# Routing of the first token block in 8 work units instead of 16, of the second with its row products in 64 instead of 56, and the wait for a zero fill moved behind other work

## The reference, cut to what matters

```python
q = (xt @ w_q).reshape(T, PEER_HEADS, 2, PEER_HALF)
s = jnp.einsum('thpd,hpkd->thpk', q, sub_keys)            # 8 heads x 2 x 128 keys a token
sv, si = lax.top_k(s, 16)
cand = sv[:, :, 0, :, None] + sv[:, :, 1, None, :]        # 16 x 16 candidates a head
top, f = lax.top_k(cand, 16)
experts, gates = (i1 * 128 + i2), softmax(top)            # 128 picks a token
h = gelu(einsum('tkd,td->tk', u[experts], x))             # u, v: 16384 rows of 1024
out = einsum('tk,tkd->td', gates * h, v[experts])
```

## Time and profile before

| | |
|---|---|
| median of 3 runs | 2676.51 us (2668.55 to 2679.03) |
| the profiled execution | 2672.81 us, its span 2671.0 us |
| PE busy | 2488.9 us, 93% |
| DVE busy | 2032.5 us, 76% |
| ACT busy | 1162.2 us, 44% |
| POOL busy | 991.8 us, 37% |
| the chain that ended last | PE 53%, DVE 23%, "issue" 11%, DMA 7%, ACT 3% |
| DMA over the span | 684.60 MB, mean 256 GB/s |

### The profile page before, as it was taken

One profiled execution on the slowest core, in us unless ns is written; L12 is line 12 of the kernel. 1 busy time (PEld: TensorE's weight loads), 2 busy tenths in 40 slices (PEclk: granted clock), 3 DMA queues, 4 the chain that ended last, 5 costly groups with the idle time before them and its releaser, 6 DMA issues.

```text
span 2671.0 us, 44784 instructions
## 1 busy us (share of the span) xinstructions
PE 2488.9 (93%) x16674; PEld 2408.7 (90%) x16674; DVE 2032.5 (76%) x3708; ACT 1162.2 (44%) x1933; POOL 991.8 (37%) x667
## 2 busy tenths in 40 slices
PE   6998998889999899999999899898999999999997
PEld 6978998889999889999999799798999999999997
DVE  3544687889987499999965467789898955777764
ACT  3444543335466333333344545333363743333332
POOL 0012007878783123333020210378888801222200
PEclk8999999999999999999999999999999999999998
DMA  7395259986966999999843633699869589999871
GB/s 311 118 303 180 89 185 367 353 280 146 235 161 197 329 403 391 381 394 377 306 166 120 148 114 133 239 345 359 236 169 231 131 278 360 349 336 353 330 281 68
DMA packets 303733, 684.60 MB, mean 256 GB/s; under 512 B 87696, under 2 KB 219664, under 8 KB 258512
## 3 DMA queue, kind: packets, MB, share of 16 engines
q1 hardware_dynamic: 218880, 496.32, 53.5%
q0 software_dynamic: 84688, 186.16, 22.5%
HBM read 595.36 MB, written 86.64 MB: 255 GB/s over the span
## 4 chain that ended last, share of the span: by engine, by line
PE 53%; DVE 23%; issue 11%; DMA 7%; ACT 3%; POOL 1%; SPq 1%; DVEq 0%; POOLq 0%; ACTq 0%
PE ps L1096 19%; PE ps L1037 16%; PE ps L869 10%; DVE u_lo L1756 5%; DMA act_scratch<-act_h 4%; DVE u_rows_s L1768 2%; DVE acc_s L2021 2%; DVE v_lo L1996 2%; DVE mod_p L2062 2%; DMA act<-act_scratch 2%; PE ps L891 1%; PE ps L1061 1%; ACT u_hi L1318 1%; DVE w L2005 1%; PE ps L976 1%
## 5 line engine op out<-in xcount | busy, mean ns | idle before, releaser
L1037 PE MATMUL ps<-h_lo,u_hi 128*128 128x320 f32 x2048 | 648.7, 317 | 70.6 <-DVE u_lo L1756 61.3
L1096 PE MATMUL ps<-w_hi,v_lo 128*128 128x320 f32 (+1 forms) x2048 | 642.8, 314 | 40.8 <-DVE v_lo L1996 36.4
L1096 PE MATMUL ps<-w_hi,v_hi 128*128 128x320 f32 x2048 | 636.5, 311 | 0.0
L1096 PE MATMUL ps<-w_lo,v_hi 128*128 128x320 f32 x2048 | 636.5, 311 | 0.0
L1037 PE MATMUL ps<-h_hi,u_hi 128*128 128x320 f32 x2048 | 635.9, 311 | 0.0
L1037 PE MATMUL ps<-h_hi,u_lo 128*128 128x320 f32 x2048 | 635.8, 310 | 0.0
L751 POOL DMA_INDIRECT gate_scratch<-scat x256 | 514.3, 2009 | 87.7 <-issue 75.3
L1388 ACT CAST v_hi<-wring 128x1024 fp32r<-128x1024 f32 x256 | 268.5, 1049 | 510.1 <-PE ps L1096 504.3
L1037 PEld LDWEIGHTS ps<-h_lo,u_hi 128*128 128x128 f32 x2048 | 387.2, 189 | 95.3 <-DVE u_lo L1756 80.0
L1096 PEld LDWEIGHTS ps<-w_hi,v_lo 128*128 128x128 f32 x2048 | 387.9, 189 | 52.5 <-issue 34.5
L1996 DVE TENSOR_TENSOR v_lo<-wring,v_hi 128x1024 fp32r<-128x1024 f32 x256 | 313.0, 1223 | 156.4 <-ACT v_hi L1388 156.3
(11 more groups left out here) (275 smaller groups left out, 3548.6 us busy)
## 6 DMA issues: line engine op xcount, KB each, us to landing
wring<-in_u_t_dram SPq DMA_DIRECT2D x128, 1024.0 KB
wring<-in_v_t_dram SPq DMA_DIRECT2D x128, 1024.0 KB
act_scratch<-act_h SPq DMA_DIRECT2D x256, 160.0 KB
gate<-gate_scratch SPq DMA_DIRECT2D x64, 640.0 KB
act<-act_scratch SPq DMA_DIRECT2D x64, 640.0 KB
wring<-in_w_ada_dram SPq DMA_DIRECT2D x24, 1024.0 KB
mod_w<-in_w_mod_dram POOLq DMA_DIRECT2D x24, 1024.0 KB, 7.8
wring<-in_w_in_dram SPq DMA_DIRECT2D x20, 1024.0 KB
```

Of the source, the lines that this page charges most:

```text
L1037: last = nc.tensor.matmul(ps[:, 6 + s % 2, 0:TD], u[:, s % 2, k], hx[:, k, 0:TD], start=(k == 0 and n == 0), stop=(k == KC - 1 and n == 2))
L1096: last = nc.tensor.matmul(ps[:, half * (KC // 2) + c, cols], v[:, of % 4, d], w[:, group * G + of, cols], start=(opening and k == 0), stop ...
```

## The change

`ROUTE_LEN` goes from (16, 56, 24) to (8, 64, 24): the first block's remaining labels have 8 splits between them, one to two labels, and the second block's 24 labels have 64. `TB_AT` follows, the other constants are derived. The dots no longer start with the split of step 2 of the second block (two there, then one a step with a second one at every sixth); they start with step 6 and go evenly over 58 steps, one a step with a second one at steps 15, 25, 34, 44, 54 and 63. POOL's wait for the zero fill moves from before `o_evac` to right before the first additions, behind the first 16 gathers.

```diff
-ROUTE_LEN = (16, 56, 24)
-TB_AT = (0, 2, 10)
+ROUTE_LEN = (8, 64, 24)
+TB_AT = (0, 1, 10)
...
-ROUTE_DOTS = tuple((s >= 2) + (s % 6 == 5) + (s == 2) for s in range(ROUTE_LEN[1]))
+DOTS_FROM = 6
+ROUTE_DOTS = tuple((s + 1 - DOTS_FROM) * SLOTS // (ROUTE_LEN[1] - DOTS_FROM) - max(s - DOTS_FROM, 0) * SLOTS // (ROUTE_LEN[1] - DOTS_FROM)
+                   if s >= DOTS_FROM else 0 for s in range(ROUTE_LEN[1]))
...
-            pool.wait_ge(nought_st.sem, nought_st.at(l, 32 * PIECES))
-            pool.sem_inc(pool_passed.sem, 1)
             pool.wait_ge(o_evac.sem, o_evac.at(l, NU))
             pool.sem_inc(pool_passed.sem, 1)
             pool.dma_start(sk_0[:], subkeys_t[l, 0]).then_inc(sk_ld.sem, 16)
...
+            pool.wait_ge(nought_st.sem, nought_st.at(l, 32 * PIECES))
+            pool.sem_inc(pool_passed.sem, 1)
             for half in range(2):
                 cells_in_two(half)
```

## The result

The changed kernel takes 2692.97 us (median of 12 executions, 2682.44 to 2707.87) against 2676.93 for the kernel before beside it: ratio 1.007, 95% interval 1.0056 to 1.0083. It is slower by 16 us; the forecast was 2674, and its range ended at 2688. The profiled execution took 2682.44 (span 2680.6) and was the fastest of the twelve. Its span is only 9.6 us longer than the span before, so part of the loss isn't in it.

What follows compares the result with a forecast made beforehand. PE was taken as the bound, kept waiting in places by DVE's work. Terms -9.0 - 20.6 + 25.1 - 2.8 + 2.0 + 3.2 = -2.1 us took the median from 2676.5 to about 2674; range 2660 to 2688.

Steps and rivals of the forecast that it cites:

- First block in 8 units: First block: DVE decides, 47.8 us for 8 units instead of 28.2; +25.1 us over both layers.
- First dots: Second block: DVE's wait for gathered rows before the first dot goes, -10.8 and -9.8, together -20.6 us.
- Residue: Second block: unexplained 5.5 and 1.9 us (restarts, clock, store waits) carried over, 1.0 a layer added; +2.0 us.
- Label stalls: Second block: PE's stalls behind long routing pieces and second dots, 19.3 us before, 17.9 after; two layers -2.8 us.
- Clock: First block: PE's idle waits lower its clock, 1.6 us a layer at the last unit; +3.2, between 0 and 5.2.
- Rival 1: Second block: DMA is the real bound and work is only conserved; +24 us, 2700; chance 0.12.
- rival 2: Second block: gathers spread over more units relieve the stores, residue and clock cost vanish; -14.7 us, 2662; chance 0.11.
- rivals 3 and 4: 3: POOL's sk_0 issue stalls anyway, +9.0 us, chance 0.05; 4: rows late for first dots, +10 us, chance 0.07.
- Zero fill: Layer 0 before unit 0: POOL's additions end earlier, PE idles 0.9 us, not 8.01; with 1.7 of clock, -9.0 us.
- Behind the second block: Gate units after the second block: no change counted, 0 us.
- Profiled execution to median: Whole kernel: the median lies 3.7 us over the profiled execution, so 2670.7 becomes about 2674.

Runs made afterwards that it cites:

- e14: Kernel after with thin gathers (each moves an eighth of the row) and a ring of 8 gathered rows instead of 16; 2663.99 us.
- e1: The kernel after, unchanged, run and profiled once more; 2696.09 us, ratio 1.0084 to the kernel before.
- e3: Kernel after with the zero fill's wait back at its old place, so only the new unit split and later dots; 2702.01 us.
- e8: Kernel after with 104 extra matmuls a layer, results unused, filling PE's waits in the first block; 2701.01 us.
- e12: Kernel after with thin rows: each gather moves 512 bytes a partition, an eighth of the row, read eight times by the dot; 2679.53 us.
- e16: Kernel after, whole rows and ring of 16, first 16 gathers in two halves: the ninth waits until unit 15 is split; 2685.53 us.
- e4: Kernel before (16 and 56 units, fill's wait at its old place) with dots from step 6 of the second block; 2686.48 us, ratio 1.0041.
- e2: Kernel before with only the wait for the zero fill moved; 2668.07 us, ratio 0.9976.
- e18: Kernel before (16 and 56 units) with the fill's wait moved and dots from step 4, 16 gathers in a row, not halved; 2656.71 us.
- e5: Kernel after with a ring of 8 gathered rows instead of 16; 2685.49 us, ratio 1.0038.
- e7: Kernel before (16 and 56 units) with the fill's wait moved, dots from step 6 and a ring of 8; 2672.78 us, ratio 0.9981.
- e17: Kernel before (16 and 56 units) with fill's wait moved, dots from step 4, first 16 gathers in two halves (ninth waits for unit 22's split); 2654.48 us.
- e10: e2 with gathers from the fifth on spaced, each waiting for a further 0.75 unit to be split; 2688.64 us, ratio 1.0053.

## Why the prediction was wrong

The median is 19 us over the forecast. Unit 0 comes 3.5 us later than forecast, units 0 to 72 take 3.3 more in the two layers (298.7 for 299.1, 299.2 for 295.5), the gate units behind them 2.4, all the rest of the span 2.5, and the median lies 10.5 over the profiled execution, not 3.7: 6.8 more. Step by step:

- **First block in 8 units, +25.1: right.** The 8 units took 47.9 us, the forecast was 47.8; with 8 units at the floor it makes 76.1, as e14's unit 16 shows (76.2 and 76.1). DVE decides there.
- **First dots, -20.6: right as far as it went.** DVE's wait is gone and the rows were there in time. (The first gather starts 6.9 us behind the end of the staging; the 7.1 of the text counts from the start of its last copy, and the sum uses 6.9.) But before, PE stood still for much of the time in which the 16 gathers ran; now it runs on beside them, and what that costs was left to the residue.
- **Residue, +2.0: the step that failed**, at "I carry these over and add 1.0 a layer". 6.5 and 2.9 us were set aside for clock, restarts and stores. With thin rows and a ring of 8 the 64 units take 241.0 (e14), in the profiled execution of the kernel after 250.8 and 251.3: the gathers' bytes and their row cost 9.8 and 10.3, which is 10.7 more in the two layers than was set aside. In e1, e3, e8 and e12 units 12 to 16 take 21.6 to 24.6 us in six of eight layers, where the first profile has 18.5. Between the medians of the kernel after and e14 lie 29 us: 13.4 go with the bytes (to e12) and 15.5 with the row (e12 to e14), or, the other way round, 7.4 with the row (to e16) and 21.5 with the rest. By e4 the later dots alone, with what they bring, are 10.8 us slower.
- **Label stalls, 17.9 a layer: too many.** 241.0 is 15.7 over the floor of 225.3. This and the clock hid 7.6 of the 10.7. The sum also slips: three times 1.17 is 3.5, which makes 18.1 and a term of -2.4.
- **Clock, +3.2: nothing.** The granted clock was 0.86 and 0.93, but unit 8 came when DVE let it, with PE kept busy too (e8). The rule of the Trainium skill weighed there (TensorE: Matmul & The Clock Gate, HAM oscillation) does show: the granted clock of these eight units is under 1.00 in both layers, and in e1 matmuls behind a wait take 0.63 us instead of 0.31. In the first block it has no price.
- **Rival 1** had the right sign and the right place, the DMA engines beside the first gathers, but not by conserved work: the 64 units took 251 us and not the 264 it gives. PE's late counts it didn't have at all. Of the others, rival 2 had the sign wrong, and rivals 3 and 4 did not come: POOL's wait went, and the rows were in time.
- **Zero fill, -9.0: 5.5** in the profiled execution (unit 0 at 327.7, before 333.2), 6.3 in e2, 7.6 in the medians. The wait went; the seven additions took 2.5 us longer, and the 1.7 of clock was not won.
- **Behind the second block, 0: +2.4.** The double dot at step 63 makes the first gate units 1.2 us a layer longer.
- **Profiled execution to median, 3.7: 10.5.** The profile shown was the fastest of twelve. Units 12 to 16 of layer 1 took 18.5 us in it and 24.6 in e1's, so late counts that differ between executions may be why; for the executions without a profile it isn't shown.

The Trainium skill (DMA: Bandwidth & Descriptors, Issuing engines are not separate DMA queues) has the DMAs of all queues interleave on the same 16 engines. The trace agrees for the stores: with an eighth of the gathered bytes ACT's waits for them went from 41.4 us to none in layer 0. It says nothing of PE's counts, which stayed late with an eighth of the bytes.

**What stays open.** Why PE's count comes late. By more than 1 us it came late only while, or right after, a row of gathers was issued, by more with 16 in a row than with 8, whatever they move. A row of 16 isn't enough for it, since e18 and one layer of e2 and e4 have one and no late count, and a row of 8 doesn't rule it out (e5, e7). PE also pauses inside units ("issue", 0.95 to 1.31 us) near such places, so the count may be late because PE itself is held up in a way the profile doesn't show; or it has to do with the recording, since all these profiles lack updates. A kernel with 8 and 64 units and 16 in a row with a whole trace would decide that, and there is none. Nor is it shown why units 10 to 13 of the kernel after are hit in every profile and units 19 to 21 of the kernel before in half of them.

## What to carry to other kernels

A wait that stands where a burst of transfers runs may be what protects the other engines from it: before taking it away, ask what would run beside the burst, and try fewer bytes or a shorter burst at the same time. That isn't always a win: halving took 7.4 us off the kernel after (e16) and nothing with 16 and 56 units (e17 against e18), and spacing cost 20.6 where rows then came late (e10). Move such work by small steps and time each: the dots from step 4 win 11 us over step 2 (e18 against e2), from step 6 they lose 10.8 (e4). And run the changed kernel more than once before believing its profile: here the first one was the fastest of twelve.

## What the hardware did that I had not expected

- PE's semaphore count reached ACT up to 12.3 us after PE's last matmul (e8, unit 11 of layer 1), in every profile of a kernel with 16 indirect DMAs in a row behind the short first block, also when each moved only 64 KB (12.2 and 15.4 us a layer, e12), and up to 2.7 us with 8 in a row (e5). All profiles that show it lack some semaphore updates, so a part of the recording in it is not ruled out.
- The same seven additions on POOL took 10.32 us where PE, DVE and ACT worked beside them, and 7.81 where PE and DVE stood still. Busy time of that stretch in the kernel after (DVE 6.52, ACT 6.18 of 10.4 us), then of two of its additions, one beside ACT alone, one beside PE, DVE and little of ACT:

```profile
234.50:244.90 10.40, 7.94 (x45) 7.30 (x43) 6.52 (x9) 6.18 (x11) 9.46 (x7) 1.00 0.68 227
...
242.71:243.71 1.00, 0.00 (x0) 0.00 (x0) 0.00 (x0) 0.93 (x1) 0.99 (x1) 1.00 0.00 0
235.70:237.52 1.82, 1.82 (x12) 1.82 (x12) 1.82 (x2) 0.28 (x1) 1.81 (x1) 1.00 0.93 335
```

and in the kernel before (DVE 0, ACT 0.98 of 7.9):

```profile
242.60:250.50 7.90, 0.00 (x0) 0.00 (x0) 0.00 (x0) 0.98 (x1) 6.95 (x7) 0.76 0.21 66
```

It isn't ACT: beside its cast alone one addition took 1.00 us, beside nothing 0.99. It isn't PE: in layer 1 six of the seven take 1.01 us with PE busy throughout. The two longest, 1.82 and 2.06 us, are those that run mostly beside DVE's split of a weight block (L1511), which took 1.75 and 1.23 us. DVE's additions and products of 128x128 (L1504, L1517) don't lengthen the ones of layer 1.
